# Depthwise taps in halves, and five of them on VectorE

## The reference, cut to what matters

```python
h = a * jax.nn.sigmoid(gate)
h = lax.conv_general_dilated(h, conv_w, window_strides=(1,), padding=[(CONV_WIDTH - 1, 0)],
                             dimension_numbers=('NWC', 'WIO', 'NWC'),
                             feature_group_count=D_C) + conv_b
h = layer_norm(h, ln_g, ln_b)
return jax.nn.silu(h)
```

```python
idx_score = jnp.where(causal[None], idx_score, -jnp.inf)
_, sel = lax.top_k(idx_score, topk)
```

## Time and profile before

| | |
|---|---|
| median of 3 runs | 1005.19 us (1004.57 to 1006.03) |
| the profiled execution | 1005.54 us |
| its span, first to last instruction | 1003.6 us |
| TensorE busy | 912.2 us (91%) |
| VectorE busy | 695.6 us (69%) |
| ScalarE busy | 560.6 us (56%) |
| GpSimd busy | 370.0 us (37%) |
| mean granted TensorE clock | 0.964 |

### The profile page before, as it was taken

How to read it: one execution, slowest core, us unless ns; L and a number is a source line. 1 busy time by engine, 2 the same in 40 slices (tenths; PEclk the granted TensorE clock), 3 DMA queues, 4 the chain that set the end, 5 groups by cost and what they waited for, 6 DMA issues and landing times.

```text
span 1003.6 us, 15909 instructions
## 1 busy us (share of the span) xinstructions
PE 912.2 (91%) x4804; PEld 715.4 (71%) x4805; DVE 695.6 (69%) x1028; ACT 560.6 (56%) x805; POOL 370.0 (37%) x243
## 2 busy tenths in 40 slices
PE   6999999999798789999936999999999999999980
PEld 5877888744366567888825888888878888888760
DVE  5339888798899956636677767798888854334276
ACT  4256667686687566611141656778777744234342
POOL 0000079999999992000001112122232221111136
PEclk9999999999899999999978999999999999999995
DMA  8550111000000100242685679999999987652375
GB/s 234 135 141 22 42 43 64 1 0 2 1 1 1 44 1 22 93 151 69 256 335 210 214 221 330 383 400 403 384 403 396 391 293 248 199 146 43 107 243 206
DMA packets 63486, 172.54 MB, mean 172 GB/s; under 512 B 19297, under 2 KB 33633, under 8 KB 51120
## 3 DMA queue, kind: packets, MB, share of 16 engines
q1 hardware_dynamic: 55664, 143.85, 38.8%
q0 software_dynamic: 7488, 27.07, 10.9%
q10 hardware_dynamic: 288, 1.05, 0.3%
HBM read 142.79 MB, written 26.74 MB: 169 GB/s over the span
## 4 chain that ended last, share of the span: by engine, by line
PE 51%; DMA 4%; DVE 3%; issue 2%; ACT 2%; POOL 1%; DVEq 0%; POOLq 0%; ACTq 0%; SPq 0%
PE ps L467 14%; PE ps L469 14%; PE ps L468 14%; DMA raw<-in_w_gate 3%; PE ps L946 2%; PE ps L819 1%; PE ps L786 1%; POOL xb L1986 1%; PE ps L982 1%; PE ps L870 1%; DMA acc_d<-ysb,idx_add 1%; PE ps L806 1%; DVE xgT_lo L1761 0%; DVE wlo L1751 0%; DMA xg<-x_d,slot_token 0%
## 5 line engine op out<-in xcount | busy, mean ns | idle before, releaser
L1751 DVE TENSOR_TENSOR wlo<-raw,whi 128x2048 fp32r<-128x2048 f32 x96 | 216.2, 2288 | 52.1 <-ACT whi L1245 52.1
L1245 ACT CAST whi<-raw 128x2048 fp32r<-128x2048 f32 x96 | 180.2, 1911 | 48.2 <-PE ps L469 18.5
L467 PE MATMUL ps<-whi,xgT_hi 128*128 128x512 f32 x384 | 152.5, 397 | 6.2 <-DVE xgT_lo L1761 6.2
L469 PE MATMUL ps<-whi,xgT_lo 128*128 128x512 f32 x384 | 150.6, 392 | 0.0
L468 PE MATMUL ps<-wlo,xgT_hi 128*128 128x512 f32 x384 | 150.2, 391 | 0.0
L1878 POOL TENSOR_SCALAR tapped<-hpad,par 128x1024 f32<-128x1024 f32 x30 | 92.0, 3067 | 2.9
L467 PE MATMUL ps<-xT_hi,w_hi 128*128 128x512 f32 (+1 forms) x224 | 88.0, 393 | 1.9 <-DVE xT_lo L1357 1.9
L1954 POOL COPY idx_now<-slot_token 128x1 int32 (+1 forms) x24 | 8.1, 336 | 219.9 <-PE ps L946 219.9
L467 PEld LDWEIGHTS ps<-whi,xgT_hi 128*128 128x128 f32 x384 | 72.7, 189 | 22.4 <-issue 6.4
L468 PE MATMUL ps<-xT_lo,w_hi 128*128 128x512 f32 (+1 forms) x224 | 86.7, 387 | 0.0
L469 PE MATMUL ps<-xT_hi,w_lo 128*128 128x512 f32 (+1 forms) x224 | 86.6, 387 | 0.0
(11 more groups left out here) (328 smaller groups left out, 1818.4 us busy)
## 6 DMA issues: line engine op xcount, KB each, us to landing
raw<-in_w_gate SPq DMA_DIRECT2D x32, 1024.0 KB, 10.4
raw<-in_w_up SPq DMA_DIRECT2D x32, 1024.0 KB, 11.7
raw<-in_w_down SPq DMA_DIRECT2D x32, 1024.0 KB, 9.4
w_raw<-in_w_in SPq DMA_DIRECT2D x14, 512.0 KB, 3.9
x_tok<-in_x SPq DMA_DIRECT2D x8, 512.0 KB, 7.7
wo_raw<-in_w_o SPq DMA_DIRECT2D x16, 256.0 KB, 2.8
x_res<-in_x SPq DMA_DIRECT2D x16, 256.0 KB, 3.4
x_d<-xa SPq DMA_DIRECT2D x4, 512.0 KB, 6.1
```

Of the source, the lines that this page charges most:

```text
L467: pe.matmul(out, l_hi, r_hi, start=start, stop=False)
L469: return pe.matmul(out, l_lo, r_hi, start=False, stop=stop)
L1245: act.copy(whi[:, n, :], raw[:, n, :]).then_inc(gu_hi if n < 4 else dn_hi, 1)
L1751: dve.tensor_tensor(wlo[:, n, :], raw[:, n, :], f32(whi[:, n, :]), ALU.subtract).then_inc(gu_lo if n < 4 else dn_lo, 1)
```

## The change

Two things are changed in who does which taps and how.

GpSimd's taps from the sixteenth on (`HALVES_FROM = 15`, tap numbers from 0) are done in halves of 512 columns: two multiplies, then two adds, each waiting only for what it needs of the same half. All of GpSimd's taps of the first group are done so too.

Of the first group's seven taps beyond TensorE's 24, VectorE takes five (`TAPS_DVE = 5`, taps 26 to 30), one at the end of each of the turns 24 to 28, into a buffer `extra`: the first is a `tensor_scalar`, the others a `scalar_tensor_tensor` that multiplies and adds to `extra`. GpSimd does taps 24 and 25, waits for `extra`, and adds it to `conv` in two halves.

Semaphores: `conv1` now counts both groups, two for each tap and for the adding of `extra`, and its end is 2 x (31 + 2 + 1) = 68; `tap_mul` counts the multiplies; `conv0_rest` and `last_done` are gone, the latter's count goes to `both_in`.

```diff
+TAPS_DVE = 5
+HALVES_FROM = 15
...
+        if p in range(len(PAIRS) - 3 - TAPS_DVE, len(PAIRS) - 3):
+            steps.append(("tap", p - (len(PAIRS) - 3 - TAPS_DVE)))
...
+        extra = at("extra", [P, S], F32, R2 + 28)
...
                 elif kind == "cm":
                     _, c, r = step
-                    pe.wait_ge(conv0_rest, TAPS - TAPS_PE)
-                    pe.wait_ge(conv1, TAPS)
+                    pe.wait_ge(conv1, 2 * (2 * TAPS - TAPS_PE - TAPS_DVE + 1))
...
+                elif kind == "tap":
+                    w = TAPS - TAPS_DVE + step[1]
+                    if step[1] == 0:
+                        dve.tensor_scalar(extra[:], hpad[:, 0, w:w + S], convw[:, w:w + 1], None, ALU.mult).then_inc(extra_set, 1)
+                    else:
+                        dve.wait_ge(extra_set, step[1])
+                        dve.scalar_tensor_tensor(extra[:], hpad[:, 0, w:w + S], convw[:, w:w + 1], extra[:], ALU.mult, ALU.add
+                                                 ).then_inc(extra_set, 1)
...
                 if w == 0:
-                    pool.tensor_scalar(conv[:, 1, :], src, by, convb[:, 1:2], ALU.mult, ALU.add).then_inc(conv1, 1)
+                    pool.tensor_scalar(conv[:, 1, :], src, by, convb[:, 1:2], ALU.mult, ALU.add).then_inc(conv1, 2)
+                elif w < HALVES_FROM:
+                    pool.wait_ge(conv1, 2 * w)
+                    pool.tensor_scalar(tapped[:], src, by, None, ALU.mult).then_inc(tap_mul, 2)
+                    pool.wait_ge(tap_mul, 2 * w)
+                    pool.tensor_tensor(conv[:, 1, :], conv[:, 1, :], tapped[:], ALU.add).then_inc(conv1, 2)
                 else:
-                    pool.wait_ge(conv1, w)
-                    link(pool.tensor_scalar(tapped[:], src, by, None, ALU.mult))
-                    pool.tensor_tensor(conv[:, 1, :], conv[:, 1, :], tapped[:], ALU.add).then_inc(conv1, 1)
+                    for c in range(2):
+                        half = slice(c * 512, (c + 1) * 512)
+                        pool.wait_ge(conv1, 2 * w - 1 + c)
+                        pool.tensor_scalar(tapped[:, half], src[:, half], by, None, ALU.mult).then_inc(tap_mul, 1)
+                    for c in range(2):
+                        half = slice(c * 512, (c + 1) * 512)
+                        pool.wait_ge(tap_mul, 2 * w - 1 + c)
+                        pool.tensor_tensor(conv[:, 1, half], conv[:, 1, half], tapped[:, half], ALU.add).then_inc(conv1, 1)
...
-            for n, w in enumerate(range(TAPS_PE, TAPS)):
-                link(pool.tensor_scalar(tapped[:], hpad[:, 0, w:w + S], convw[:, w:w + 1], None, ALU.mult))
-                pool.tensor_tensor(conv[:, 0, :], conv[:, 0, :], tapped[:], ALU.add).then_inc(conv0_rest, 1)
-                pool.wait_ge(conv0_rest, n + 1)
+            for n, w in enumerate(range(TAPS_PE, TAPS - TAPS_DVE)):
+                for c in range(2):
+                    half = slice(c * 512, (c + 1) * 512)
+                    pool.wait_ge(conv1, 2 * (TAPS + n) - 1 + c)
+                    pool.tensor_scalar(tapped[:, half], hpad[:, 0, w + c * 512:w + (c + 1) * 512], convw[:, w:w + 1],
+                                       None, ALU.mult).then_inc(tap_mul, 1)
+                for c in range(2):
+                    half = slice(c * 512, (c + 1) * 512)
+                    pool.wait_ge(tap_mul, 2 * (TAPS + n) - 1 + c)
+                    pool.tensor_tensor(conv[:, 0, half], conv[:, 0, half], tapped[:, half], ALU.add).then_inc(conv1, 1)
+            pool.wait_ge(extra_set, TAPS_DVE)
+            for c in range(2):
+                half = slice(c * 512, (c + 1) * 512)
+                pool.wait_ge(conv1, 2 * (2 * TAPS - TAPS_PE - TAPS_DVE) - 1 + c)
+                pool.tensor_tensor(conv[:, 0, half], conv[:, 0, half], extra[:, half], ALU.add).then_inc(conv1, 1)
```

More of the change, by code:

```diff
@@ L422, in program @@
             sem(n) for n in ("diag_set", "conv0_mm", "conv0", "conv1", "pooled", "pool_chain"))
-        conv0_rest, both_in, both_mm = sem("conv0_rest"), sem("both_in"), sem("both_mm")
+        tap_mul, both_in, both_mm = sem("tap_mul"), sem("both_in"), sem("both_mm")
         ring_mm, ring_act, ring_dve = sem("ring_mm"), sem("ring_act"), sem("ring_dve")
@@ L458, in program @@
         rows_in = [sem(f"rows_in{i}") for i in range(2)]
-        ln_rstd, last_done = sem("ln_rstd"), sem("last_done")
+        ln_rstd, extra_set = sem("ln_rstd"), sem("extra_set")
         ln2_in, fin_done, out_done = sem("ln2_in"), sem("fin_done"), sem("out_done")
@@ L1141, in _ @@
                     if step[1] == 0:
-                        act.wait_ge(conv0_rest, TAPS - TAPS_PE)
-                        act.wait_ge(conv1, TAPS)
+                        act.wait_ge(conv1, 2 * (2 * TAPS - TAPS_PE - TAPS_DVE + 1))
                         act.wait_ge(ring_act, seen(RING_ACT, RING_OF["pw", 1, 1]))
@@ L1838, in _ @@
             dve.scalar_tensor_tensor(xc[:], xc[:], rstd2[:, (NT + 1) % 2:(NT + 1) % 2 + 1], ln2_b[:], ALU.mult, ALU.add
-                                     ).then_inc(last_done, 1)
+                                     ).then_inc(both_in, 1)
         @block.gpsimd
@@ L1907, in _ @@
             pool.wait_ge(conv0, 1)
-            pool.wait_ge(conv1, TAPS)
-            for n, w in enumerate(range(TAPS_PE, TAPS)):
-                link(pool.tensor_scalar(tapped[:], hpad[:, 0, w:w + S], convw[:, w:w + 1], None, ALU.mult))
-                pool.tensor_tensor(conv[:, 0, :], conv[:, 0, :], tapped[:], ALU.add).then_inc(conv0_rest, 1)
-                pool.wait_ge(conv0_rest, n + 1)
+            pool.wait_ge(conv1, 2 * TAPS)
+            for n, w in enumerate(range(TAPS_PE, TAPS - TAPS_DVE)):
[13 more added lines that the diff above has]
+                pool.tensor_tensor(conv[:, 0, half], conv[:, 0, half], extra[:, half], ALU.add).then_inc(conv1, 1)
             pool.wait_ge(searched, 1)
@@ L2004, in store_rows @@
                 else:
-                    pool.wait_ge(last_done, 1)
+                    pool.wait_ge(both_in, 4)
                 pool.wait_ge(out_done, 16 * NT)
```

## The result

The changed kernel takes 992.25 us as the median of 4 runs (991.12 to 996.53), the kernel before 1005.31 us in 4 runs beside it (1004.57 to 1006.03). The ratio is 0.9893, with a 95% interval from 0.9867 to 0.9918. The gain is 13.1 us by the two medians and 10.7 us by this ratio. The prediction was 997.0 us, range 990.5 to 1003.5. The profiled execution took 991.12 us, with a span of 989.0 us and a mean granted clock of 0.970.

A forecast was written before the change was run, and what follows sets the result against it. VectorE, waiting inside selection instructions for GpSimd's taps, was taken to pace the attention until 359 us, then TensorE. Terms -3.0 - 0.8 - 6.2 + 1.6 + 0.6 + 0.1 - 0.5 = -8.2 us took 1005.2 to 997.0 us, range 990.5 to 1003.5.

The forecast's parts named there:

- Halves halve the waits: VectorE's top-k selection: 26.6 us of waits for running GpSimd instructions halve, 13.3 us less on VectorE.
- By stage: Attention from 254 to 382 us, in three stages: gains of 3.0, 0.8 and 6.2 us, before the price of VectorE's taps.
- the clock: TensorE's granted clock during the attention: shorter gaps prevent some lower-level time, 0.5 us gained, bounds 0 and 5.2.
- rival 1: VectorE's selection: halves halve the waits for GpSimd, 5 to 11 us gained, 994 to 1000 us; chance 0.60.
- rival 2: Attention: waits go nearly away and TensorE's clock holds, 12.8 us gained, 992.4 us; chance 0.14.
- Half taps of 5.8 us: GpSimd's taps in halves: 5.8 us each where whole ones take 5.38, its own 18 ending at 361 us.
- Rival 3: Conv means: GpSimd becomes the end from 6.4 us a tap; at 7.2, 6.6 us slower, 1012 us; chance 0.10.
- Five taps, 1.6 + 0.6 + 0.1: VectorE's taps after pairs 24 to 28: first costs 1.6 us, second 0.6, third and fourth nothing, last 0.1.
- GpSimd's last add within 3 us behind VectorE's last tap: End of the taps on GpSimd: its buffer adds finish within 3 us of VectorE's last tap, before TensorE's conv means.
- The renamed and merged semaphores cost nothing: Tap semaphores: no cost, since no instruction is added and GpSimd's order was serial already.
- The means at 373 to 376 us: Attention's end, TensorE's conv means (L841): at 373 to 376 us, where it was 382.52.

The follow-up runs named there:

- alone: Changed kernel with GpSimd's taps from the sixteenth on left out: 117.4 us from the pooling's second column to the conv means, against 133.6 before; whole time not comparable.
- Neutral: Kernel before with only the change's semaphore counting, raised by 4 for each whole multiply and add: 1006.63 us, 1.0033 times before.
- repeat: The changed kernel itself, timed and profiled again beside the follow-up kernels: 995.26 us, 0.9909 times the kernel before.
- Halves_only: Kernel before with the change's semaphores and GpSimd's taps in halves from the sixteenth on, none moved to VectorE: 1013.46 us, 1.0091 times before.
- Quarters: Changed kernel with GpSimd's taps in quarters of 256 columns where it has halves: 1009.68 us, 1.0051 times the kernel before.
- no_five: Changed kernel without VectorE's five taps and the adding of their buffer: 122.7 us from pooling's second column to conv means, against 123.4; whole time not comparable.

## Why the prediction was right, step by step

- **The bound was rightly read.** VectorE paced the attention by waiting for GpSimd; without the taps the stretch shrinks by 16.2 us (alone).
- **"Halves halve the waits", -13.3 us**: mechanism right, term too small. The waits fell by 17.5 us, to 38.3 us of selection where 42 was forecast. "No longer than its own work plus 1.3 us" held: most beyond its own work is the 1.72 us of L1487 over 384 columns (266.44 us, own work 0.47); the scan's 3.25 us over 1024 has 1.0 beyond its 2.25. Neutral alone had 6 us less of waits too. Its whole taps have the 0.17 us gaps, the changed kernel's half taps have none, so the gaps are no part of the halves' effect; whether the gaps let VectorE in was not tested by itself.
- **By stage**: -3.0, -0.8 and -3.9 (-6.2 with the taps' +2.3 to set against it) were forecast, -0.5 for the clock besides. Measured, clock and taps included: -3.2, -1.3 and -5.6, then -0.1. The sum was -8.2 and is -10.2 (-10.5 on repeat). Three terms were off, and partly cancelled. The taps' price was too large: 0.4 to 0.7 for 2.3. The clock was too small: the work lost to it fell by 3.4 us (5.2 to 1.8), where 0.5 was taken out of bounds of 0 to 5.2. The relief from waiting was too large: TensorE's idle time in the three stages fell by 6.5 us, 6.9 to 7.2 without the taps' price, where 10.0 was forecast. That is so although VectorE's own waits fell by more than forecast, in the third stage by 8.9 us for 6.2. The split between clock and waiting is from the stage rows; no run separates them. That the stages came out near is therefore in part luck.
- **Which rival.** 992.25 us lies outside the 994 to 1000 of rival 1, the one held likeliest, and on the 992.4 of rival 2, held at 0.14. The repeat, 995.26 us, and the stretch's 10.2 us lie within rival 1. The mechanism lies between the two: a third of the waits stayed, not half and not nothing, and a third of the loss to the clock.
- **Half taps of 5.8 us**: 5.55 undisturbed. But VectorE, getting in more often, delays GpSimd more: from its sixteenth tap at 244.54 to 362.11 its 18 taps took 117.6 us, 99.9 by their own work and 17.7 of delay, where 11 was forecast. The two errors cancelled to 2 us (115.4 forecast). Halves_only tells the same: 143.7 us for 23 taps, 16 of it delay. Rival 3's threshold of 6.4 us a tap was thus too high: with 17.7 us of delay and the means at 369.4, GpSimd would be late from 5.8 us a tap on, just the price that the forecast had taken. That the half tap came out at 5.55 kept rival 3 away, by 0.25 us a tap. Quarters, at 6.4, are over the threshold either way; halves_only is late by having five taps more.
- **Five taps, 1.6 + 0.6 + 0.1**: 0.4 to 0.7 us (no_five). VectorE in the changed kernel is less pressed than in the trace of before, from which I priced them (it is busy 90% of the third stage, with the first tap and part of the second in it, where it was 94%). The Trainium skill's doubt (Perfetto Trace Analysis, section Optimizing Scalar/DVE Operations) about moving work between the two engines did not hold here: they took some 25 us off GpSimd (5 taps of 5.55, less 2.5 for adding the buffer) for that price.
- **GpSimd's last add within 3 us behind VectorE's last tap, ready 2.2 us ahead of the means**: 2.6 and 2.3 us.
- **"The renamed and merged semaphores cost nothing"**: wrong. Whole taps on them take some 0.15 us more each, which made neutral 1.0033 times before; the rows point to counts that go up by more than 1, not to the number of waits, which is the same. The changed kernel hides it, as its GpSimd waits for VectorE at the end anyway; in front of the sixteenth tap it is 1.5 us.
- **The means at 373 to 376 us**: 369.4. Of the miss below 373, 2.9 us are the early start, a difference between executions, and the forecast has no share in them. Some such difference may be in the 992.25 us too; on repeat the gain was 9.1 us by the ratio (0.9909), close to the stretch.

## What to carry to other kernels

When two engines wait for each other inside their instructions, take the shortest row of each kind as its work, sum the rest as waits, and find which of the other engine's instructions a wait ends with: only those need to be shorter, and only as far as the other engine's own end allows. Relief on one side is paid in part on the other, so move work off the engine that pays in the same step. Compare stretches between two events that both kernels share before reading a difference of spans, and lay the windows so that they hold the same work. Read TensorE's granted clock in the same rows as its waits: here it was about a third of the gain.

## What was not expected of the hardware

- GpSimd's multiply over 128x1024 float32 takes 2.84 us undisturbed with one operation and scalar, 1.19 with two (mean of 37: 1.34); halves 1.53 and 0.76 us. Why the longer form is faster is open.
- Short GpSimd instructions in a row held a 6-column VectorE instruction for 14.45 us, whereas in the changed kernel VectorE gets in between two half adds (the rows at 330 us). What decides it stays open. Halves_only, which differs in the second operation of the multiply alone (1.53 us for 0.76 a half), had no such hold, but its operations of 6 columns came before its halves; neither was varied further.
- With semaphores raised by 2 or 4 in place of 1, each whole instruction of GpSimd that waits for the one before it starts some 0.07 us later (gaps of 0.15 and 0.17 us for 0.08 and 0.10), 0.15 us a tap. That the step of the count is the cause fits the rows above, but it wasn't varied by itself.
- Two executions of the same kernel differed by 3.0 us ahead of the first tap (130.6 and 127.6 us), with 133.6 us each in the stretch.
